# Expert results by way of DRAM: six scatter products replaced by stored rows, one gather and transposes

## What is computed

```python
logits = (a @ router).astype(jnp.float32)
top_v, top_i = lax.top_k(logits, TOP_K)            # TOP_K = 2
top_w = jax.nn.softmax(top_v, axis=-1)
gate = jnp.sum(jax.nn.one_hot(top_i, N_EXPERTS) * top_w[..., None], axis=-2)
out = jnp.zeros_like(a)
for e in range(N_EXPERTS):
    h = jax.nn.silu(a @ w_gate[e]) * (a @ w_up[e])
    out = out + gate[..., e:e + 1] * (h @ w_down[e])
```

## Time and profile before

| | |
|---|---|
| median of 3 runs | 1281.48 us (1278.38 to 1283.33) |
| the profiled execution's own time | 1278.62 us |
| its span, first to last instruction | 1276.7 us |
| PE busy | 1191.6 us, 93% |
| PE weight load busy | 981.8 us, 77% |
| DVE busy | 471.1 us, 37% |
| ACT busy | 282.0 us, 22% |
| POOL busy | 205.0 us, 16% |
| chain that ended last, by engine | PE 86%, DVE 5%, issue 3%, ACT 2%, DMA 2% |
| data moved | 330.06 MB, mean 259 GB/s |
| mean granted PE clock | 0.979 of full speed |

### The profile page before, as it was taken

The page is one execution under the profiler, slowest core; times in us unless marked ns, Lnnn a source line. Parts: engine busy times, 40 slices in busy tenths (PEclk is TensorE's granted clock), DMA queues, the critical chain, the costliest instruction groups (busy, mean ns, idle before and its releaser), DMA issues.

```text
span 1276.7 us, 37806 instructions
## 1 busy us (share of the span) xinstructions
PE 1191.6 (93%) x15722; PEld 981.8 (77%) x15722; DVE 471.1 (37%) x1367; ACT 282.0 (22%) x757; POOL 205.0 (16%) x344
## 2 busy tenths in 40 slices
PE   7999999999999998998786879989899999999998
PEld 5887886999999976675344547787878977878976
DVE  2110114677774332003757674233211311212213
ACT  1000003110010022134867763121010110110122
POOL 3022132021340000223444541010000000000000
PEclk9999999999999998998989899999999999999999
DMA  9786869998443374564556876499999999989831
GB/s 308 294 321 244 316 242 336 152 392 306 139 159 116 149 280 149 169 105 132 182 178 222 263 232 237 158 387 385 399 363 379 360 360 379 349 341 380 318 124 37
DMA packets 109644, 330.06 MB, mean 259 GB/s; under 512 B 15816, under 2 KB 34201, under 8 KB 107812
## 3 DMA queue, kind: packets, MB, share of 16 engines
q1 hardware_dynamic: 91156, 263.86, 56.5%
q0 software_dynamic: 17168, 63.50, 16.3%
q10 hardware_dynamic: 1152, 0.30, 0.1%
HBM read 319.16 MB, written 15.70 MB: 262 GB/s over the span
## 4 chain that ended last, share of the span: by engine, by line
PE 86%; DVE 5%; issue 3%; ACT 2%; DMA 2%; POOLq 0%; POOL 0%; ACTq 0%; DVEq 0%
PE bank L1975 20%; PE bank L2591 15%; PE bank L2077 12%; PE pbank L2602 6%; PE bank L2113 6%; PE bank L2031 5%; PE pbank L2591 3%; PE bank L2602 3%; PE bank L2181 2%; DMA gring<-in_moe 1%; PE bank L2543 1%; PE bank L2208 1%; PE bank L2348 1%; PE bank L2303 1%; PE pbank L2543 1%
## 5 line engine op out<-in xcount | busy, mean ns | idle before, releaser
L2591 PE MATMUL bank<-X,gring 128*64 128x96 f32 x4608 | 197.0, 247 | 5.5 <-issue 5.5
L2591 PEld LDWEIGHTS bank<-X,gring 128*64 128x64 f32 x4608 | 193.0, 138 | 10.1 <-issue 10.1
L1975 PE MATMUL bank<-aT,gring 128*128 128x288 f32 x768 | 193.0, 410 | 3.5 <-DVE aT L1306 3.5
L1975 PEld LDWEIGHTS bank<-aT,gring 128*128 128x128 f32 x768 | 146.6, 192 | 46.2 <-issue 5.6
L2602 PE MATMUL pbank<-Q,X 128*32 128x256 f32 x1152 | 75.3, 379 | 0.0
L2077 PE MATMUL bank<-aT,gring 128*128 128x144 f32 x528 | 72.0, 286 | 0.0
L2031 PE MATMUL bank<-Q,X 128*64 128x64 f32 x2048 | 63.3, 223 | 7.7 <-issue 7.7
L2031 PEld LDWEIGHTS bank<-Q,X 128*64 128x64 f32 x2048 | 61.3, 138 | 11.7 <-issue 11.3
L1901 DVE TENSOR_TENSOR X<-X,bank 128x96 f32<-128x96 f32 x72 | 18.4, 256 | 134.5 <-ACT X L1252 132.6
L2077 PEld LDWEIGHTS bank<-aT,gring 128*128 128x128 f32 x528 | 67.7, 190 | 0.0
L1894 DVE TENSOR_TENSOR hT<-hT,bank 128x288 f32<-128x288 f32 x48 | 18.9, 448 | 128.5 <-PE bank L2543 128.5
(11 more groups left out here) (387 smaller groups left out, 1779.3 us busy)
## 6 DMA issues: line engine op xcount, KB each, us to landing
gring<-in_moe SPq DMA_DIRECT2D x176, 512.0 KB, 5.9
Q<-in_moe SPq DMA_DIRECT2D x72, 512.0 KB, 7.1
gring<-in_dense_gu SPq DMA_DIRECT2D x44, 512.0 KB, 14.1
Q<-in_cache_cmp POOLq DMA_DIRECT2D x64, 256.0 KB, 5.6
Q<-in_cache_cmp SPq DMA_DIRECT2D x64, 256.0 KB, 5.3
gring<-in_conv_in SPq DMA_DIRECT2D x24, 512.0 KB, 10.8
gring<-in_dense_down SPq DMA_DIRECT2D x16, 704.0 KB, 5.4
gring<-in_ple_gate SPq DMA_DIRECT2D x16, 512.0 KB, 6.2
```

The source lines that it names most:

```text
L1975: ins = pe.matmul(bank(label, k)[:, 0:T], tile[:, 128 * i:128 * i + 128], rhs[:, i, :], start=i == 0, stop=i == C - 1)
L2591: ins = pe.matmul(m_bank(i, M_GU + f)[64 * w:64 * w + 64, CAP * u:CAP * u + CAP], gslot(("m", 0), 2 * f + u)[:, o:o + 64], ae[:, c, :], st ...
```

## The change

For experts 0 to 5 (`STORED` = 6) the scatter, the `scat` matrices and the adds to `hT` are gone from items 1 to 6. In place of them:

- after the three copies to `ye`, ACT issues four DMAs (`rows_kept`) that store the item's 96 result rows in a DRAM tensor `expert_rows` (32 partitions x 3 x 256 floats each); row 0 of it holds zeros;
- DVE works out once, in item 0 after f = 5, for each token the numbers of its up to two rows and their gate weights (`out_numbers`, 13 small operations);
- in item 6 POOL waits until all 24 stores have landed and fetches both rows of each token, in three groups of 128, 128 and 32 tokens (`rows_out`, six indirect DMAs); DVE weighs and adds them (`rows_added`, after f = 5, 7 and 9); PE transposes the sums between its gate and up and its down (`rows_transposed`, 24 transposes into eight banks); DVE adds the banks to `hT` (`sums_added`).

Experts 6 and 7 still go by scatter, in the loop and after it. Items 0 to 5 now take 16 places each, and item 6 has its eight transposed banks at places 13 to 20.

```diff
@@ POOL, after the fetches of items' rows
+            pool.wait_ge(slots_ready, 5)
+            m_full(pool, FIXED - 1, 1)
+            pool.wait_ge(stored, 16 * 4 * STORED)
+            for g in range(3):
+                n = 128 if g < 2 else 32
+                for k in range(2):
+                    pool.indirect_dma_start(rows_out[g][k][0:n, :], None, expert_rows[:, :],
+                                            bass.IndirectOffsetOnAxis(ap=out_index[0:n, 2 * g + k:2 * g + k + 1], axis=0)).then_inc(gathered[k], 16)
@@ ACT
                 for t in range(3):
                     m_full(act, i, M_DOWN + t)
+                    if t == 0 and isinstance(i, int) and i:
+                        act.wait_ge(stored, 16 * 4 * i)
                     m_drain(act.activation(ye[:, t, :], m_bank(i, M_DOWN + t)[:, 0:256], ACT.Copy), i, M_DOWN + t)
+
+            def rows_kept(i):
+                for t in range(3):
+                    m_drained(act, i, M_DOWN + t)
+                for j in range(4):
+                    dst = expert_rows[1 + CAP * i:1 + CAP * i + CAP, 256 * j:256 * j + 256]
+                    act.dma_start(dst.rearrange("(t r) n -> r t n", r=32), ye[32 * j:32 * j + 32, :, :]).then_inc(stored, 16)
 
             for i in range(FIXED):
                 expert_acts(i)
+                if i < STORED:
+                    rows_kept(i)
@@ DVE
+            def rows_added(g):
+                n = 128 if g < 2 else 32
+                a, b = rows_out[g]
+                for k in range(2):
+                    dve.wait_ge(gathered[k], 16 * (3 + 3))
+                chain(dve.tensor_scalar(a[0:n, :], a[0:n, :], out_gates[0:n, 2 * g:2 * g + 1], None, ALU.mult))
+                settled()
+                dve.scalar_tensor_tensor(a[0:n, :], b[0:n, :], out_gates[0:n, 2 * g + 1:2 * g + 2], a[0:n, :],
+                                         ALU.mult, ALU.add).then_inc(picks_ready, 1)
+
+            def sums_added():
+                i = FIXED - 1
+                for k in range(C):
+                    h = hT[:, scattered(k), :]
+                    m_full(dve, i, M_SUM + k)
+                    m_drain(dve.tensor_tensor(h, h, m_bank(i, M_SUM + k)[:, 0:T], ALU.add), i, M_SUM + k)
...
-                    if f == 5:
+                    if f == 5 and isinstance(i, int) and i == 0:
                         dve.wait_ge(slots_in, 16 * 2)
+                        row_numbers()
+                        out_numbers()
+                    if isinstance(i, int) and i == FIXED - 1 and f in (5, 7, 9):
+                        rows_added(f // 2 - 2)
+                    if f == 5 and not (isinstance(i, int) and i < STORED):
                         for t in range(3):
...
+            item_table()
             for i in range(FIXED):
-                if i:
-                    expert_adds(i)
-                else:
-                    item_table()
                 expert_products(i, i, 0)
+            sums_added()
@@ PE
+            def rows_transposed(i):
+                pe.wait_ge(picks_ready, 6)
+                for k in range(C):
+                    m_free(pe, i, M_SUM + k)
+                    c = scattered(k)
+                    for g in range(3):
+                        n = 128 if g < 2 else 32
+                        ins = pe.transpose(m_bank(i, M_SUM + k)[:, 128 * g:128 * g + n], rows_out[g][0][0:n, 128 * c:128 * c + 128],
+                                           ident[0:n, 0:n])
+                    m_fill(ins, i, M_SUM + k)
+
             def expert_matmuls(i):
...
-                if not (isinstance(i, int) and i == 0):
+                if not isinstance(i, int):
                     for t in range(3):
                         m_drained(pe, i - 1, M_DOWN + t)
-                    pe.wait_ge(scat_ready, 3 * i)
+                    pe.wait_ge(scat_ready, 3 * i - 3 * STORED)
                     scatter(i)
...
+                if isinstance(i, int) and i == FIXED - 1:
+                    rows_transposed(i)
                 for t in range(3):
                     m_free(pe, i, M_DOWN + t)
```

More of the change, by code:

```diff
@@ L83 @@
 MB = PS + 2
+M_SUM = MR
+STORED = FIXED - 1
 VALUES_AT = [(), (0, 1), (2,), (3,)]
@@ L462, in m_place @@
         def m_place(i, k):
-            return k - C if isinstance(i, int) and i == 0 and k >= M_SCAT else k
+            if not isinstance(i, int) or k < M_SCAT:
+                return k
+            if i == FIXED - 1 and k >= M_SUM:
+                return M_GU + FC - C + k - M_SUM
+            return k if i == FIXED - 1 and k >= M_DOWN else k - C
         def m_turn(i, k):
             if isinstance(i, tuple):
-                return MR // MB * i[0] - 1
-            return m_place(i, k) // MB if isinstance(i, int) and i == 0 else MR // MB * i - 1 + k // MB
+                return MR // MB * i[0] + 1 - (MR // MB - 2) * FIXED
+            if isinstance(i, int):
+                return 2 * i + m_place(i, k) // MB
+            return MR // MB * i + 1 - (MR // MB - 2) * FIXED + k // MB
         m_base = RES[("pg", 1, 0)] - 2
@@ L582, in item_count @@
             eng.wait_ge(items_ready, 1)
[L583 to L584 removed]
+            extra = eng.value_load(items[0:1, 2 * NI:2 * NI + 1], min_val=1, max_val=NI - FIXED)
+            return extra, eng.value_load(items[0:1, 2 * NI + 1:2 * NI + 2], min_val=1, max_val=NI - FIXED) + FIXED - 2
         def item_value(eng, row, i, top):
@@ L1240, in _ @@
                 tokens(k)
-            act.wait_ge(item_cleared, 1)
+            act.wait_ge(item_cleared, 2)
             def expert_acts(i):
@@ L1888, in row_numbers, with out_numbers @@
                 dve.tensor_copy(row_index[0:CAP, 1:FIXED], row_number[0:CAP, 1:FIXED]).then_inc(slots_ready, 1)
+            def out_numbers():
+                p1 = pos1[:, :, 0:STORED]
+                chain(dve.scalar_tensor_tensor(out_row, p1, float(CAP) + 0.5, p1, ALU.is_lt, ALU.mult))
+                settled()
+                chain(dve.scalar_tensor_tensor(out_hit, out_row, 0.0, first_row.unsqueeze(1).to_broadcast([128, 3, STORED]),
+                                               ALU.is_gt, ALU.mult))
+                settled()
+                chain(dve.tensor_tensor(out_row, out_row, out_hit, ALU.add))
+                settled()
+                chain(dve.tensor_reduce(out_sum, out_row, AX.X, ALU.add))
+                rows, gates = (t.rearrange("p (i k) -> p i k", k=2) for t in (out_rows, out_gates))
+                chain(dve.tensor_reduce(rows[:, :, 0], out_row, AX.X, ALU.max))
+                settled()
+                chain(dve.tensor_tensor(rows[:, :, 1], out_sum, rows[:, :, 0], ALU.subtract))
+                settled()
+                for k in range(2):
+                    chain(dve.tensor_tensor(out_hit, out_row, rows[:, :, k].unsqueeze(2).to_broadcast([128, 3, STORED]), ALU.is_equal))
+                    settled()
+                    chain(dve.tensor_tensor(out_hit, out_hit, rg[:, :, 0:STORED], ALU.mult))
+                    settled()
+                    chain(dve.tensor_reduce(gates[:, :, k], out_hit, AX.X, ALU.add))
+                    settled()
+                dve.tensor_copy(out_index[:, :], out_rows).then_inc(slots_ready, 1)
@@ L1922, in item_table @@
                 settled()
-                for j, n in enumerate((EXPERTS - FIXED, EXPERTS - 2)):
+                for j, n in enumerate((EXPERTS - FIXED, EXPERTS - FIXED)):
                     chain(dve.tensor_scalar(items_f[:, 2 * NI + j:2 * NI + j + 1], okey[:, 0:1], float(n), None, ALU.add))
@@ L2616, in _ @@
                 m_drained(pe, more + 1, M_DOWN + t)
-            pe.wait_ge(scat_ready, 3 * more + 6)
+            pe.wait_ge(scat_ready, 3 * more + 6 - 3 * STORED)
             scatter((more + 2,))
@@ L2652, in constants @@
     k["slot_of_row"] = np.arange(1, 129, dtype=f)[:, None]
+    k["first_row"] = np.tile(CAP * np.arange(STORED, dtype=f), (128, 1))
     k["token_number"] = np.tile(np.arange(T, dtype=f), (128, 1))
```

35 lines of the change are left out of this document (21 added, 14 removed).

## The result

| | before | after |
|---|---|---|
| median of four runs each, us | 1279.93 (1276.64 to 1283.33) | 1296.72 (1296.39 to 1297.79) |
| profiled execution's own time, us | 1278.62 | 1296.92 |
| its span, us | 1276.7 | 1295.2 |
| PE busy, us | 1191.6 | 1188.7 |
| DVE busy, us | 471.1 | 452.4 |

The change makes the kernel slower: ratio 1.0132, 95% interval 1.0103 to 1.0162, 16.8 us between the medians. The forecast was 1291 us in a range of 1279 to 1300. The direction and the range held; the size didn't, 16.8 us against 9.3.

What follows compares the result with a forecast made beforehand. PE was taken to set the pace from item 2, DMA engines close behind. Boundaries -3.1, clock +8.5, transposes +2.5 and third sum +1.4 gave +9.3 us on the 1281.5 us median: 1291 us, range 1279 to 1300.

Steps and rivals of the forecast that it cites:

- Four are 1.93 us ... the copies to `ae` queue behind them: Item boundaries: ACT's four store issues delay its copies and PE, leaving 0.52 us gained per boundary, -3.1 us in all.
- I expect the fall after five of the six boundaries: +8.5: Boundaries: 2.6 us of PE idle halves the clock for 3.4 us, costing 1.7 us each; +8.5 us, bounds 0 and 10.2.
- PE loses time that nothing in the profile explains ... I let it stand as it is: Gate and up: PE's unexplained loss, 5.5 us on that line of the chain, was taken to stay unchanged.
- 24 in 2.84 us; with the short ones I take +2.5: Item 6: 24 added transposes, a third of 32 tokens, add 2.5 us to PE, bounds 2.0 and 2.9.
- PE waits for the third sum, +1.4: Item 6, after gate and up: PE waits for DVE's third sum, +1.4 us with semaphores, bounds 0.4 and 5.5.
- The stores ... fit, just: Items 2 to 6: 4.7 MB of stores and fetches, 12 us, fit in 14.6 us of DMA idle, costing nothing.
- SP's price: Boundaries, rival: ACT issues at SP's lower price, idle 2.1 us, clock mostly holds; -0.5 us, 1281 us, chance 0.12.
- issues free: Boundaries, rival: store issues don't hold ACT's copies, gate and up start at 1089.69, no clock lost; 1271 us, chance 0.10.
- DMA engines become the limit: Item 6, rival: rows come latest or weight tiles queue behind fetches; +19 us, 1301 us, chance 0.10.

Runs made afterwards that it cites:

- the busy gap: Changed kernel with ten useless PE products behind the transposes of each boundary of items 1 to 6; 1290.2 us, ratio 1.0078.
- the run with whole transposes: Changed kernel with the third token group's transposes taking 128 rows instead of 32; 1295.74 us, ratio 1.0114.
- POOL's plain copies: Changed kernel with item 6's six indirect fetches replaced by same-size plain copies from fixed addresses, still issued by POOL; one run, 1292.98 us.
- paced fetches: Changed kernel with the six indirect fetches issued one after each f = 1 to 6 of item 6, a semaphore per token group; 1294.34 us, ratio 1.0099.
- the stores by themselves: Kernel before, all scatter products kept, with only the 24 stores added, issued by POOL and read by nobody; 1281.05 us, ratio 1.0012.
- neither stores nor fetches: Changed kernel without the 24 stores and six fetches, with third transposes of 128 rows; 1277.37 us, ratio 0.9988.
- all repairs with stores and fetches: Changed kernel with paced fetches and 128-row third transposes; stores by ACT behind its copies to `ae` 1280.29 us, 1.0002, or by POOL 1283.06 us, 1.0017.
- POOL's stores: Changed kernel with the 24 stores issued by POOL instead of ACT, nothing else moved; 1284.95 us, ratio 1.0045.

## Why the prediction was right in direction, and too small

- **"Four are 1.93 us ... the copies to `ae` queue behind them"**: right. ACT's issues took 0.31 and three times 0.45 us, the boundary was 3.41 us at item 5 where 3.42 was forecast, 3.6 on average, and with the stores on POOL, or on ACT behind the copies, the wait is gone. The gain at six boundaries was 2.2 us of the 3.1 forecast, since single issues took up to 1 us.
- **"I expect the fall after five of the six boundaries: +8.5"**: right in mechanism (the busy gap), over-sized in this profile. (Of the idle stretches between 1.9 and 2.2 us in the trace before, six of seven kept the full clock, not five of six.) The clock fell after two, once for 6.8 us and once for 3.4, that is 5 us at half of each. The five other profiles of kernels with the same gap had two, three, four, four and five falls, so the number isn't fixed by the gap's length alone. The run with the gap filled came out 6 to 7 us faster, which bounds the clock's cost in the medians roughly from above, between the 5 of this profile and the 8.5 forecast. Nor does a fall always cost half its length: in the run with whole transposes the clock was at half for 3.4 us as item 1's gate and up began, and they took 33.22 us, against 33.27 in the change without a fall there.
- **The missing term.** The forecast costed the fetches by when their rows land (a wait for the third sum), and put possible harm to PE down to late weight tiles. In the change's profile it was neither: tiles were in time in item 6, and PE was stalled while POOL issued. The profile had no burst of indirect DMAs in this stage, so nothing in the earlier trace rows said it; but no lower and upper bound was given for PE's side of the burst, and that is the step that failed. It measured 8.6 us in the profile, half clock included, and 8.7 in the medians (1296.7 to 1288.0; 3 to 13 by the intervals). By these figures it is more than the whole excess of 7.5 us over the forecast. Its form differs between executions: with the same burst item 6's gate and up took 38.0 us here and 34.6 in the run with whole transposes.
- **"24 in 2.84 us; with the short ones I take +2.5"**: mis-sized, 4.34. Short was taken for cheap. With the earlier trace rows alone, and three equal groups, it would have been right (2.77).
- **"PE waits for the third sum, +1.4"**: mis-sized, 0.24. The rows were there when DVE wanted them, as gate and up itself had been held up for 8.6 us. Where the same burst left PE going, DVE waited 5.9 and 5.1 us for the rows (2.5 were forecast) and the sum came 0.9 and 0.7 us late; it was 1.4 in the run with POOL's plain copies, and 0.2 with paced fetches. The one price that the Trainium skill gave (page "DMA: Bandwidth & Descriptors", section "Anatomy of one DMA") would have put this term at 0.4 and is nearer. That doesn't confirm it: in the run with whole transposes DVE went on with the rows 12.8 us after the last fetch's issue had ended.
- **"The stores ... fit, just"**: right for the stores by themselves (1.0012). With the scatter away it is less clear: neither stores nor fetches 0.9988, all repairs with stores and fetches 1.0002 and 1.0017, whose intervals overlap.
- **"PE loses time that nothing in the profile explains ... I let it stand as it is"**: it didn't stand. From 890 to 1185 us it was 7.1 us before and 9.4 with the change, and 9.1 to 16.4 us in the kernels with boundaries of 1.56 us. So a boundary that gets shorter by 2.4 us isn't worth 2.4 us, which the forecast's sum took for granted.
- **"SP's price", "issues free", "DMA engines become the limit"**: the first two fell with the four rows of ACTq above; the third gave 1301, close to the result, but by a share that did not come: 0.92 in items 2 to 6. The price of the second, 1271 us, was wrong as well: with all six boundaries at 1.56 us the kernel without stores and fetches came to 1277.4.

The terms as they came in the profile: boundaries -2.2, clock at boundaries +5.1, gate and up of items 1 to 5 otherwise -1.4, fetches +8.6, transposes +4.3, sums +0.2, in all +14.6. What stands in item 0 (0.9), in the looped item (1.5) and ahead of the items (1.0) isn't explained by the change; these places differ by as much among the profiles of the experiments.

Open: why the burst of indirect DMAs brings PE down to pieces of five records in two profiles (the change, POOL's stores) and not in two others with the same burst (whole transposes, gap filled). No wait stands behind these stalls.

The other stalls of kind "issue" have a trace that can be read. The page has a DMA queue for instructions (queue and kind: packets, MB, share):

```profile
q8 instruction: 123, 2.02, 0.6%
```

Each of these packets has 16 KB. Over the fourteen profiles, PE has 188 stalls of kind "issue" of 0.3 us or more in gate and up and in down between 892 and 1236 us; 181 of them ended 1.2 to 1.65 us after such a packet had been moved, and the seven others are all from the pieces of five records. The stalls in a row lie 127 or 128 matmul records apart, in the change's item 1 after 285, 412, 539 and 666. The busy gap added 20 records per boundary, and there they stand after 265, 392, 519 and 646; in item 6 after 342 and 469, where the kernels with plain or paced fetches have them after 461 and 588. So they go by the place in PE's instructions and not by its data: PE waits for its own instructions. In the change's item 1 PE restarts every 6.1 us, while 127 records take 5.5 us, so there this supply sets the pace. That it is also why gate and up grow as the boundaries get shorter, since PE then comes sooner to the next packet, is argued from this and not isolated by a run.

## What to carry to other kernels

Work that is taken off the busiest engine is worth only what the next limit leaves: find out first with a kernel that leaves it out and puts nothing in its place (here 0.9988, so the whole idea had 0.1% to give, and by the interval 0.3% at most). An edit that puts DMA issues on a computing engine belongs behind the last instruction of that engine that somebody waits for; four issues ahead of two copies cost here 2 us per boundary and some of the clock; behind them the boundary was 1.56 us. Where a burst of DMAs is added, bound its price for the engine that sets the pace, and not only for the engine that reads the data. And before trusting one profile of a stage, look for the same stage in a second: item 6 came in two forms here.

## What the hardware showed that was not expected

- Six indirect DMAs of 128 rows or fewer, issued by POOL back to back (0.86 to 0.96 us each), stood beside a PE that did five matmul records in 1.45 us in two profiles, though it waited for none of their data, and beside a PE at its normal pace in two others. Leaving them out made the kernel some 8 us faster.
- PE's stalls that the profile calls "issue" ended, in 181 of 188 cases, 1.2 to 1.65 us after a packet of 16 KB on the instruction queue, 127 or 128 matmul records apart where they come in a row.
- 24 transposes took 4.34 us with a third of them of 32 rows, and 2.77 us with all of 128 rows.
- The clock's fall after a gap isn't a matter of the gap alone: 2.5 to 2.8 us kept 1.00 at four boundaries and 2.5 us lost it at a fifth.
